# Rotary query columns of all heads projected ahead of the heads, plain query columns two heads at a time

## The chip, the cores and the metric

The kernel runs on one core of one Trainium2 chip. The metric is device microseconds for one execution, the lower the better. The core's engines are TensorE (PE, with PEld for its weight loads), VectorE (DVE), ScalarE (ACT), GpSimd (POOL) and SyncE (SP), which issues most DMAs. Each engine runs its own instructions in its own order, and they wait for one another by semaphores that count up.

## What is computed

The reference is one inference step of a two-layer decoder, for a prompt of 512 + 16 meta tokens and for 8 running samples of 4 new tokens each: 560 tokens in all. The first layer's mixer is multi-head latent attention with 16 heads, and only it is touched by the change:

```python
z = x @ w_in                                   # 1024 -> 384 + 256 + 32
cq = rms_norm(z[..., :384], q_norm)
ckv = rms_norm(z[..., 384:640], kv_norm)
kr = rope(z[..., 640:], pos)                   # one rotary key for all heads
q = (cq @ w_q_up).reshape(B, L, 16, 64 + 32)   # per head: 64 plain, 32 rotary columns
q_rope = rope(q[..., 64:], pos)
q_lat = einsum('blhn,chn->blhc', q[..., :64], w_uk)
s = (q_lat . c_kv + q_rope . k_rope) * 96 ** -0.5   # causal, then softmax, then times c_kv
```

`rope` takes the two halves x1, x2 of 32 columns to (x1 cos - x2 sin, x2 cos + x1 sin). The samples attend to 1024 cached positions, eight pages of 128 rows per sample, found through a page table. After the attention come its output projection, a SwiGLU channel mixer, an RG-LRU mixer and a second SwiGLU; they take the larger part of the time, and the change does not touch them.

## The kernel before

Activations are kept transposed, features on partitions and the 560 tokens along the row, in two halves of 280 (`toks`, `TH`). Products that need float32 precision are made as three fast products: operand and weight are each split into a rounded part and a remainder (`zqh`, `zql`; `wqh`, `wql`).

The attention of the prompt works by pairs of heads p = 0..7, each with a first head (u = 0) and a second head (u = 1). `pe ... head(p, u)` (L1155) is the order of TensorE's work, written out by hand: the scores of each block of 128 query rows (`scores`, L1071; block 4 is that of the 16 meta-end rows of both heads), transposes of earlier probabilities (`turn`, L1093), the products with the values of the head before (`outputs`, L1111), and, put in between, the projections for heads to come: `keys` (L1047), and `queries` (L1060), 18 matmuls of 280 columns per head: two token halves by three 128-row slices by three products. `queries` makes for one head a tile of 128 rows: 64 plain ones, the 32 rotary ones, and the same 32 once more with their halves swapped:

```python
# GpSimd, swap (L2725): the weights' halves swapped, then split
pool.tensor_copy(wq[u][:, :, 96:112], wq[u][:, :, 80:96]).then_inc(wq_sw, 1)
pool.tensor_copy(wq[u][:, :, 112:128], wq[u][:, :, 64:80]).then_inc(wq_sw, 1)
```

VectorE's `read_q` (L2194) multiplies the lower 64 rows by `trig` (cos and signed sin, scaled), ScalarE's `read_q` (L1668) copies the plain rows with the scale and, for the sample tokens, into `Qs`. `Q[u]` then holds 128 rows, and its product with `K[u]` (64 plain key rows, and the rotated rotary key `krs` twice) sums up the score in one matmul. The weights of a head's queries are loaded by SP into one of two tiles `wq[0]`, `wq[1]`, so that one can be loaded and split while the other is in use.

SP's program is one list. Around the attention it is: the loads of the front; the pages of samples 0 and 1 and the rotary pages of sample 0, as soon as VectorE's parameter steps are done (L574); after that the numbers of pages 2 and 3; the pages of sample 2; `pair_weights(0)` (L586), which waits for TensorE's transpose of `wuk` (`wt_sum`) and for each `queries` (`q_sum`) and loads the next pair's weights; the pages of sample 3; and then a loop with `pair_weights(i)` and the rotary pages of one sample (`sample_ropes`, L565) in each step. `numbers(b)` (L555) loads eight page numbers from SBUF into registers, once before each set of page loads. After the loop come the pages of samples 4 to 7.

GpSimd's list, in the heads: `values` (L2734) copies a head's values, `rotary` (L2738) gathers the sample columns of `Q`, `swap` prepares query weights, `key_weights` (L2744) key weights, `rows_out` (L2712) stores the latent rows, with four DMA issues for two tiles.

After the last head, TensorE needs the gathered sample queries (`qrot`) spread by a small matmul with `spread` (L1233), and it transposes the cached pages (`fill`, L1134). `fill(0, 4)` is the first to need rotary pages, and waits until those of all eight samples have come (`in_rp`).

Of the kernel before, what the change touches and what calls it, by code (L numbers as in the profile page):

```python
# [15 lines left out]
F32 = mybir.dt.float32  # L16
# [7 lines left out]
P = 128  # L24
# [107 lines left out]
def trunk(nc, x_prompt, x_sample, cache_latent, cache_krope, page_table, state_lru_h, state_conv, meta_tokens,  # L132
          mla_w_in, mla_q_norm, mla_w_q_up, mla_kv_norm, mla_w_uk, mla_w_uv, mla_w_o,
          lru_w_in, lru_conv_w, lru_conv_b, lru_w_a, lru_b_a, lru_w_i, lru_b_i, lru_lambda, lru_w_o,
          ffn_w_gu, ffn_w_down, ln_g, ln_b, c_ident, c_trig, c_mask, c_smask,
# [3 lines left out]
    with ExitStack() as ctx:  # L139
# [58 lines left out]
        wq = [put(f"wq{s}", [P, KQ, P]) for s in range(2)]  # L198
# [8 lines left out]
        rt = put("rt", [32, 2, T])  # L207
# [14 lines left out]
        wql = [place(f"wql{s}", [P, KQ, P], F32R, wq_at + 4 * KQ * P * s)[0] for s in range(2)]  # L222
        wqh = [place(f"wqh{s}", [P, KQ, P], F32R, raw_at + 4 * (PAGES * KV_R + KQ * P * s))[0] for s in range(2)]
# [6 lines left out]

        Ctok = [put(f"Ctok{s}", [P, PAGES, KV_R]) for s in range(2)]
        RP = put("RP", [P, B, PAGES, ROPE])
        Ctok += [raw[s][:, 0:PAGES * KV_R].rearrange("p (n c) -> p n c", n=PAGES) for s in range(2)]
# [9 lines left out]
        spt = put("spt", [P, 6, KD])  # L243
        zn = put("zn", [P, KC, NS])
# [246 lines left out]
        def _(sp):  # L491
# [41 lines left out]
            sp.dma_start(trig[:], c_trig).then_inc(in_att, 16)  # L533
# [13 lines left out]
            for u in range(2):  # L547
                sp.dma_start(wq[u][:, :, 0:hw], wqv[:, :, hw * u:hw * u + hw]).then_inc(wq_in[u], 16)
            for r in (64, 96):
                sp.dma_start(spread[r:r + 32, :].rearrange("p (a c) -> p a c", a=4),  # L550
                             c_ident[0:32, 0:32].rearrange("p (a c) -> p a c", a=1).broadcast_to([32, 4, 32])
                             ).then_inc(in_att, 16)
# [22 lines left out]
            sp.wait_ge(in_pg, 16)  # L575
            for b in range(2):
# [8 lines left out]

            def pair_weights(i):  # L586

                for u in range(2):
                    if u == 0:
                        sp.wait_ge(wt_sum, i + 1)  # L590
                        sp.dma_start(wuk[:], wukv[:, :, bass.ds(i * P + P, P)]).then_inc(wuk_in, 16)
                    sp.wait_ge(q_sum, i * 2 + (u + 1))
# [2388 lines left out]
```

## Time and profile before

| | |
|---|---|
| time, median of 3 runs | 1311.28 us (1310.70 to 1313.13) |
| the profiled execution's own time | 1310.86 us |
| its span, first to last instruction | 1309.0 us |
| TensorE busy | 1290.5 us, 99% of the span |
| VectorE busy | 883.3 us, 67% |
| ScalarE busy | 619.5 us, 47% |
| GpSimd busy | 279.5 us, 21% |
| granted TensorE clock, mean | 0.999 |

Busy times are for one execution. The heads lie between about 73 and 235 us; what follows the attention begins at about 300 us. In the profile's rows a line begins with its start and length in us, then engine, line of the kernel, operation, the tile written and those read, the shape and the number of instructions merged; in brackets stands the idle time of the engine before it and what ended it. "PE ps L1066" means TensorE writing to the accumulator memory for line 1066. A busy TensorE has overlapping matmuls, so a matmul's own length is more than the distance to the next.

### The profile page before, as it was taken

The page shows a single profiled execution, that of the slowest core. Times are in us where ns is not written, and L with a number is a line of the kernel's source. Part 1 is how long each engine was busy: PE and PEld are TensorE (multiplying, and loading weights), DVE is VectorE, ACT ScalarE, POOL GpSimd, SP SyncE. Part 2 cuts the span into 40 slices and gives each one's busy share as a digit, 9 for nine tenths or more (in the row PEclk, how much of TensorE's full clock was granted, in tenths as well). Part 3 has the DMA queues.
Part 4 walks back from the last instruction along what each step waited for, and adds up shares of the span by engine and source line. Part 5 has one row for each costly group of instructions (what it writes and reads, how often), then busy time and mean ns, then how long its engine had stood idle before and what let it go on. Part 6 is the DMA issues. An engine that isn't in the chain of part 4 may idle for free.

```text
span 1309.0 us, 26890 instructions
## 1 busy us (share of the span) xinstructions
PE 1290.5 (99%) x9985; PEld 1215.5 (93%) x9985; DVE 883.3 (67%) x1326; ACT 619.5 (47%) x1061; POOL 279.5 (21%) x391
## 2 busy tenths in 40 slices
PE   9999999999999999999999999999999999999997
PEld 9877777669999999999999899999999999999997
DVE  5766676433868478478864868888784784788646
ACT  4456666332555244144433488854552441444333
POOL 1243322001510000001104415645200000111034
PEclk9999999999999999999999999999999999999999
DMA  7231110342242655557752214222425655577501
GB/s 228 69 111 26 30 30 9 97 131 65 65 129 71 153 134 139 149 124 167 172 164 73 73 37 108 65 78 85 125 74 150 140 136 149 126 162 172 176 14 69
DMA packets 210088, 139.97 MB, mean 107 GB/s; under 512 B 27096, under 2 KB 198701, under 8 KB 210000
## 3 DMA queue, kind: packets, MB, share of 16 engines
q1 hardware_dynamic: 199616, 119.11, 31.9%
q0 software_dynamic: 10384, 19.67, 9.0%
q8 instruction: 58, 0.95, 0.3%
q14 instruction: 30, 0.25, 0.1%
HBM read 116.85 MB, written 3.02 MB: 92 GB/s over the span
## 4 chain that ended last, share of the span: by engine, by line
PE 78%; DVE 7%; ACT 5%; DMA 3%; issue 3%; POOL 2%; SPq 0%; DVEq 0%; POOLq 0%; ACTq 0%
PE ps L699 23%; PE ps L738 21%; PE ps L777 6%; PE ps L842 4%; PE ps L1079 3%; PE ps L1066 3%; DMA raw<-raw 2%; DVE wl L2044 2%; DMA raw<-in_ffn_w_gu 2%; PE ps L1102 1%; PE ps L1248 1%; PE ps L1290 1%; PE ps L914 1%; PE ps L1452 1%; PE ps L1312 1%
## 5 line engine op out<-in xcount | busy, mean ns | idle before, releaser
L738 PE MATMUL ps<-Th,wh 128*128 128x280 f32 x576 | 167.9, 292 | 0.0
L738 PE MATMUL ps<-Th,wl 128*128 128x280 f32 x576 | 167.5, 291 | 0.0
L738 PE MATMUL ps<-Tl,wh 128*128 128x280 f32 x576 | 167.2, 290 | 0.0
L2847 POOL DMA_DIRECT2D raw<-raw x36 | 42.9, 1192 | 531.3 <-DMA raw<-in_ffn_w_gu 531.3
L1540 ACT ACTIVATE wh<-raw 128x2048 fp32r<-128x2048 f32 (+4 forms) x50 | 92.3, 1846 | 122.2 <-PE ps L699 112.7
L2044 DVE TENSOR_TENSOR wl<-raw,wh 128x2048 fp32r<-128x2048 f32 (+4 forms) x50 | 113.2, 2264 | 31.9 <-ACT wh L1540 31.8
L738 PE MATMUL ps<-xl,wh 128*128 128x280 f32 x432 | 126.4, 293 | 0.0
L738 PE MATMUL ps<-xh,wh 128*128 128x280 f32 x432 | 125.9, 292 | 0.0
L738 PE MATMUL ps<-xh,wl 128*128 128x280 f32 x432 | 125.7, 291 | 0.0
L699 PE MATMUL ps<-hh,wh 128*128 128x280 f32 x512 | 107.9, 292 | 1.5 <-DVE wl L2044 1.5
L738 PEld LDWEIGHTS ps<-Th,wh 128*128 128x128 f32 x576 | 108.3, 188 | 0.0
L738 PEld LDWEIGHTS ps<-Th,wl 128*128 128x128 f32 x576 | 108.2, 188 | 0.0
L738 PEld LDWEIGHTS ps<-Tl,wh 128*128 128x128 f32 x576 | 108.2, 188 | 0.0
L699 PE MATMUL ps<-hl,wh 128*128 128x280 f32 x512 | 107.7, 292 | 0.0
L699 PE MATMUL ps<-hh,wl 128*128 128x280 f32 x512 | 107.5, 291 | 0.0
L1901 ACT ACTIVATE wh<-raw 128x512 fp32r<-128x512 f32 x36 | 22.8, 633 | 130.2 <-DVE w_s L2523 127.9
L699 PEld LDWEIGHTS ps<-hh,wh 128*128 128x128 f32 x512 | 81.1, 188 | 2.0 <-DVE wl L2044 2.0
L699 PEld LDWEIGHTS ps<-hh,wl 128*128 128x128 f32 x512 | 81.5, 189 | 0.0
L738 PEld LDWEIGHTS ps<-xh,wh 128*128 128x128 f32 x432 | 81.3, 188 | 0.2 <-DVE wl L2535 0.2
L738 PEld LDWEIGHTS ps<-xh,wl 128*128 128x128 f32 x432 | 81.4, 188 | 0.0
L699 PEld LDWEIGHTS ps<-hl,wh 128*128 128x128 f32 x512 | 81.1, 188 | 0.0
L738 PEld LDWEIGHTS ps<-xl,wh 128*128 128x128 f32 x432 | 81.1, 188 | 0.0
(442 smaller groups left out, 3649.0 us busy)
## 6 DMA issues: line engine op xcount, KB each, us to landing
raw<-in_ffn_w_gu SPq DMA_DIRECT2D x140, 256.0 KB, 4.7
raw<-in_ffn_w_gu SPq DMA_DIRECT2D x36, 512.0 KB, 4.1
raw<-raw POOLq DMA_DIRECT2D x36, 512.0 KB, 5.1
raw<-in_ffn_w_down SPq DMA_DIRECT2D x48, 256.0 KB, 3.1
raw<-in_lru_w_in SPq DMA_DIRECT2D x16, 512.0 KB, 4.9
Ctok<-in_cache_latent SPq DMA_DIRECT2D x48, 128.0 KB, 2.3
raw<-in_ffn_w_down SPq DMA_DIRECT2D x16, 384.0 KB, 3.7
raw<-in_mla_w_o SPq DMA_DIRECT2D x16, 256.0 KB, 3.6
```

Of the source, the lines that this page charges most:

```text
L699: mm = pe.matmul(ps[:, 1024 * jp + 512 * h:1024 * jp + 512 * h + TH], w[:, k, col:col + P], side(x, k, h), start=(k == 0 and n == 0), stop ...
L738: mm = pe.matmul(bank_of(bank), a, b, start=(k == 0 and m == 0), stop=(k == 3 and m == 2))
L777: mm = pe.matmul(bk(at), w[:, k, col:col + P], side(x, k, h), start=(k == 0 and n == 0), stop=(k == K_ - 1 and n == 2))
L842: return pe.matmul(bk(2 * (t + s) + h), w[:, k, P * s:P * s + P], x[:, k, toks(h)], start=(k == 0 and i == 0), stop=(k == KD - 1 and i == 2))
L914: return pe.matmul(ps[:, at:at + cols.stop - cols.start], w[:, k, jp * P:jp * P + P], x[:, k, cols], start=start, stop=stop)
L1066: mm = pe.matmul(ps[:, 512 * n:512 * n + TH], w[u][:, k, :], x[:, n * TH:(n + 1) * TH], start=(k == 0 and i == 0), stop=(k == KQ - 1 and i ...
L1079: pe.matmul(ps[:, bank:bank + w], Q[u][:, P * i:w], K[u][:, 0:w], start=True, stop=False)
L1102: mm = pe.transpose(ps[:, bank + j * P:bank + j * P + P], Pr[u][:, PR_AT[i] + j * P:PR_AT[i] + j * P + P], ident[:])
L1540: act.activation(wh[u][:, start:w], raw[u][:, start:w], ACT.Copy).then_inc(hi_ok, 1)
L1901: act.activation(quarters(wh[1], 0), quarters(raw[u], 0), ACT.Copy)
L2044: dve.tensor_tensor(wl[u][:, start:w], raw[u][:, start:w], wh[u][:, start:w].bitcast(F32), ALU.subtract).then_inc(lo_ok, 1)
L2847: pool.dma_start(quarters(raw[u], 3, 2), quarters(raw[u], 0, 3)[:, 0:3:2, :], accum_op=ALU.add).then_inc(r_out, 16)
```

## The change

The rotary columns of four heads at a time (32 each, 128 rows) are projected ahead of the first head, in four groups, and kept in four tiles `ropes`. From then on a projection makes the plain columns of two heads (2 x 64 rows), once per pair: half of its matmuls in the first head of the pair before, half in the second. The rotation's halves are no longer swapped in the queries: `Q[u]` gets rows 64 to 95 as `ropes` times cos, and rows 96 to 127 as `ropes` times sin, both made by GpSimd, and the lower rows of `K[u]` hold the rotated key and the key turned by a quarter. VectorE makes this second key with four more small products. Only one `wq` tile is left. SP loads the rotary columns in 12 small DMAs into space that pages use later, so the pages of samples 0 and 1 wait for their projection (`s_zms`), and the sines share space with the last rotary pages, so the rotary pages of samples 5 to 7 wait for the last rotary step (`q_rot`).

The core of the diff (tiles' places, constants, and the changes in semaphores' counts are cut):

```diff
             sp.wait_ge(s_xt, 10)
+            for g in range(4):
+                for k in range(KQ):
+                    sp.dma_start(wr[:, g, k, :].rearrange("p (h c) -> p h c", h=4),
+                                 wqv[:, k, 4 * hw * g:4 * hw * (g + 1)].rearrange("p (h c) -> p h c", h=4)[:, :, NOPE:hw]
+                                 ).then_inc(pg_in[4], 16)
...
+            sp.dma_start(sines[:], c_trig[2 * P:3 * P, :]).then_inc(pg_in[4], 16)
             sp.wait_ge(in_pg, 16)
+            def pair_weights(i):
+
+                sp.wait_ge(q_sum, i + 1)
+                for s in range(2):
+                    sp.dma_start(wq[:, :, NOPE * s:NOPE * s + NOPE],
+                                 wqv[:, :, bass.ds(i * (2 * hw) + (2 + s) * hw, NOPE)]).then_inc(wq_in[0], 16)
+                sp.wait_ge(wt_sum, i + 1)
+                sp.dma_start(wuk[:], wukv[:, :, bass.ds(i * P + P, P)]).then_inc(wuk_in, 16)
+
+            pair_weights(0)
+            sp.wait_ge(s_zms, 6)
             for b in range(2):
                 pages_b = numbers(b)
                 sample_pages(b, pages_b)
...
             pages_23 = [numbers(b) for b in (2, 3)]
             sp.wait_ge(s_v, 8)
             sample_pages(2, pages_23[0])
...
-            pair_weights(0)
+            pair_weights(1)
             sample_pages(3, pages_23[1])
             sample_ropes(1, numbers(1))
-            with sp.Fori(1, HEADS // 2 - 1) as i:
+            sample_ropes(2, numbers(2))
+            for i in range(2, HEADS // 2 - 1):
                 pair_weights(i)
-                sample_ropes(i + 1, numbers(i + 1))
+                if i < 4:
+                    sample_ropes(i + 1, numbers(i + 1))
+            sp.wait_ge(q_rot, 3 * HEADS)
+            for b in range(5, B):
+                sample_ropes(b, numbers(b))
             pages_45 = [numbers(b) for b in (4, 5)]
...
+            def rope_queries(g, at):
+
+                for n in range(2):
+                    for k in range(KQ):
+                        for i, (w, x) in enumerate(((wrh, zqh[k][:]), (wrh, zql[:, k, :]), (wrl, zqh[k][:]))):
+                            mm = pe.matmul(ps[:, 512 * (at + n):512 * (at + n) + TH], w[:, g, k, :], x[:, toks(n)],
+                                           start=(k == 0 and i == 0), stop=(k == KQ - 1 and i == 2))
+                mm.then_inc(s_zms, 1)
...
-                    if i == 4:
-                        if last:
-                            fill(0, 0)
-                            fill(0, 1)
-                        else:
-                            queries(h + 1, v, 0)
+                    if i == 4 and last:
+                        fill(0, 0)
+                        fill(0, 1)
...
-                    if i == 3 and u == 0:
-                        queries(h + 1, v, 0)
-                if not last:
-                    if u == 1:
-                        pe.wait_ge(ql_rd, p + 1)
-                    queries(h + 1, v, 1)
-                else:
+                if u == 0 and more:
+                    queries(p + 1, 0)
+                elif u == 1 and not last:
+                    pe.wait_ge(ql_rd, p + 1)
+                    queries(p + 1, 1)
+                elif last:
                     fill(0, 2)
                     fill(0, 3)
...
+            rope_queries(0, 4)
+            pe.wait_ge(s_ve, 5)
+            pe.wait_ge(s_vd, 5)
+            rope_queries(1, 2)
+            rope_queries(2, 0)
+            pe.wait_ge(s_zroot, 8)
+            rope_queries(3, 4)
...
             def read_q(p):
+                dve.wait_ge(q_sum, p + 1)
+                dve.tensor_scalar(halves(Q[1][0:NOPE, :]), pair(0, 64, P), SCALE, None, ALU.mult)
...
+                dve.tensor_scalar(Qs[64:P, NS:2 * NS], ps[64:P, 512 + TH - NS:512 + TH], SCALE, None, ALU.mult).then_inc(q_dve, 1)
...
+            def split_queries(p):
+
+                pool.wait_ge(wq_in[0], 32 * p + 32)
+                pool.tensor_copy(wqh[:], wq[:]).then_inc(wq_sw, 1)
+                pool.wait_ge(wq_sw, 2 * p + 3)
+                pool.tensor_tensor(wql[:], wq[:], wqh[:].bitcast(F32), ALU.subtract).then_inc(wq_sw, 1)
...
+            def rotary(h):
+
+                p, u, g, rows = h // 2, h % 2, h // 4, slice(32 * (h % 4), 32 * (h % 4) + 32)
+                pool.wait_ge(s_zinv if g % 2 else s_zroot, 3 + g // 2 if g % 2 else 8 + g // 2)
+                if p > 0:
+                    pool.wait_ge(sc_sum, scored(p - 1, 1, 3 if u else 4))
...
+                pool.tensor_tensor(Q[u][64:96, :], ropes[g][rows, :], trig[rows, :], ALU.mult).then_inc(q_rot, 1)
+                pool.wait_ge(q_rot, 3 * h + 1)
+                pool.tensor_tensor(Q[u][96:P, :], ropes[g][rows, :], sines[rows, :], ALU.mult).then_inc(q_rot, 1)
+                pool.wait_ge(q_rot, 3 * h + 2)
+                pool.tensor_copy(qrot[64:P, :, h:h + 1, :].rearrange("p b a t -> p b (a t)"),
+                                 Q[u][64:P, NP:T].rearrange("p (b t) -> p b t", t=TS)).then_inc(q_rot, 1)
...
+            rotary(0)
             for t in range(2, 4):
                 rows_out(t)
+            rotary(1)
+            split_queries(1)
             key_weights(1)
             for h in range(1, HEADS):
+                if h < HEADS - 1:
+                    rotary(h + 1)
                 if h == 1:
                     for t in range(4, 6):
                         rows_out(t)
                 elif h % 2 == 0 and h < HEADS - 2:
+                    split_queries(h // 2 + 1)
                     key_weights(h // 2 + 1)
                 if h < HEADS - 1:
                     pool.wait_ge(o_sum, h * 2)
                     values(h + 1, 1 - h % 2)
```

## Rows read from the trace of the kernel before

**Rows 1.** Stretches: busy us of PE, PEld, DVE, ACT, POOL; PEclk; DMA share; GB/s.

```profile
3.00:4.00 1.00, 1.00 (x7) 1.00 (x7) 0.00 (x0) 0.00 (x0) 0.00 (x0) 1.00 0.61 168
...
8.00:9.00 1.00, 1.00 (x12) 1.00 (x11) 0.66 (x3) 0.42 (x2) 0.00 (x0) 1.00 0.99 400
...
92.00:112.00 20.00, 20.00 (x158) 15.75 (x159) 13.55 (x36) 12.78 (x39) 6.84 (x18) 1.00 0.14 31
```

**Rows 2.** The chain of waits, end of a first head and start of a second.

```profile
96.04 2.31 PE ps L1066 x18
...
99.96 0.97 PE ps L1083 x4
...
101.56 1.15 PE ps L1066 x9
```

**Rows 3.** Timeline of PE: pair 0, and the first head of pair 1.

```profile
73.32 0.46 PE L1079 MATMUL ps<-K,Q 128*128 128x128 f32 x2
...
76.66 0.38 PE L1066 MATMUL ps<-zqh,wqh 128*128 128x280 f32 x1
...
80.24 1.04 PE L1083 MATMUL ps<-K,Q 128*16 128x512 f32 x4 [0.23 <-ACT Qs L1676]
...
91.84 0.49 PE L1079 MATMUL ps<-K,Q 128*128 128x128 f32 x2
...
98.28 0.44 PE L1122 MATMUL ps<-PT,Vs 128*64 128x264 f32 x1
```

**Rows 4.** Timelines of DVE (the first row) and ACT (the other two).

```profile
49.04 1.82 DVE L2147 TENSOR_TENSOR rt<-ps,trig 32x280 f32<-32x280 f32 x4
...
97.43 0.59 ACT L1655 ACTIVATE PT<-ps 128x512 f32<-128x512 f32 x1
...
101.86 0.70 ACT L1647 ACTIVATE Pr<-ps,mx 80x528 f32<-80x528 f32 x1 [0.97 <-DVE mx L2179]
```

**Rows 5.** Timeline of POOL.

```profile
28.69 1.40 POOL L2704 TENSOR_TENSOR zsq<-zsq 128x560 f32<-128x560 f32 x1 [1.04 <-ACT zsq L1597]
...
73.67 0.54 POOL L2722 DMA_DIRECT2D out<-lat  x1 [3.36 <-ACT lat L1619]
...
91.98 0.40 POOL L2735 COPY Vs<-V 128x256 f32<-128x256 f32 x1 [6.15 <-PE ps L1131]
...
96.66 0.51 POOL L2730 CAST wqh<-wq 128x384 fp32r<-128x384 f32 x1
97.26 1.01 POOL L2732 TENSOR_TENSOR wql<-wq,wqh 128x384 fp32r<-128x384 f32 x1
```

**Rows 6.** Timeline of SP's queue: DMA issues.

```profile
41.39 4.03 SPq L562 DMA_DIRECT2D Ctok<-in_cache_latent  x8
45.61 4.40 SPq L567 DMA_DIRECT2D RP<-in_cache_krope  x8
54.62 3.95 SPq L562 DMA_DIRECT2D Ctok<-in_cache_latent  x8
67.95 4.75 SPq L562 DMA_DIRECT2D raw<-in_cache_latent  x8
74.09 0.39 SPq L591 DMA_DIRECT2D wuk<-in_mla_w_uk  x1
...
88.38 4.05 SPq L567 DMA_DIRECT2D RP<-in_cache_krope  x8
...
235.10 9.20 SPq L562 DMA_DIRECT2D Ctok<-in_cache_latent  x16
```

**Rows 7.** DMA issues from 20 to 200 us: size and median us to landing.

```profile
wq<-in_mla_w_q_up SPq DMA_DIRECT2D x16, 144.0 KB, 2.4
```

**Rows 8.** Timeline of PE: pair 7 begins; transposes of rotary pages and of pages 4.

```profile
209.85 0.49 PE L1079 MATMUL ps<-K,Q 128*128 128x128 f32 x2
...
229.63 0.60 PE L1152 MATMUL ps<-ident,RP 128*128 128x128 f32 x4
...
249.31 1.09 PE L1152 MATMUL ps<-ident,Ctok 128*128 128x128 f32 x8
```

More of the change, by code:

```diff
@@ L197, in trunk @@
         wq_at = put.at()
-        wq = [put(f"wq{s}", [P, KQ, P]) for s in range(2)]
+        wq = put("wq", [P, KQ, P])
+        put("wq_pad", [P, KQ, P])
         wuk = put("wuk", [P, KC, P])
@@ L221, in trunk @@
         zqh = [place(f"zqh{k}", [P, T], F32R, at)[0] for k, at in enumerate((stat_at, ring_end - 3072, rt_at))]
-        wql = [place(f"wql{s}", [P, KQ, P], F32R, wq_at + 4 * KQ * P * s)[0] for s in range(2)]
-        wqh = [place(f"wqh{s}", [P, KQ, P], F32R, raw_at + 4 * (PAGES * KV_R + KQ * P * s))[0] for s in range(2)]
+        wql = place("wql", [P, KQ, P], F32R, wq_at)[0]
+        wqh = place("wqh", [P, KQ, P], F32R, raw_at + 4 * PAGES * KV_R)[0]
+        ktrig = place("ktrig", [P, T], F32, qlat_at + 4 * 2 * (KV_R + ROPE))[0]
+        sines = place("sines", [P, T], F32, LIMIT - 4 * T)[0]
+        ropes = [place(f"ropes{g}", [P, T], F32, at)[0] for g, at in enumerate((
+            xh_at + 16 * T, xh_at + 4 * KD * T + 16 * T, xh_at + 20 * T, stat_at + 4 * T))]
         wuvh = place("wuvh", [P, KC, HEADS * VH], F32R, raw_at + 4 * W_MAX)[0]
@@ L229, in trunk @@
         kvh, kvl = (t[:, KD - KC:KD, :] for t in (xh, xl))
+        ctok_at = put.at()
         Ctok = [put(f"Ctok{s}", [P, PAGES, KV_R]) for s in range(2)]
+        rp_at = put.at()
         RP = put("RP", [P, B, PAGES, ROPE])
+        wr, wrh, wrl = (place(n, [P, 4, KQ, P], dt, at)[0] for n, dt, at in (
+            ("wr", F32, ctok_at), ("wrh", F32R, ctok_at + 4 * PAGES * KV_R), ("wrl", F32R, rp_at)))
         Ctok += [raw[s][:, 0:PAGES * KV_R].rearrange("p (n c) -> p n c", n=PAGES) for s in range(2)]
@@ L574, in _ @@
             sp.wait_ge(s_par, 26)
+            sp.dma_start(sines[:], c_trig[2 * P:3 * P, :]).then_inc(pg_in[4], 16)
             sp.wait_ge(in_pg, 16)
+            def pair_weights(i):
+                sp.wait_ge(q_sum, i + 1)
+                for s in range(2):
+                    sp.dma_start(wq[:, :, NOPE * s:NOPE * s + NOPE],
[4 more added lines that the diff above has]
+            sp.wait_ge(s_zms, 6)
             for b in range(2):
@@ L1158, in head @@
                 last = isinstance(h, int) and h == HEADS - 1
+                more = not isinstance(p, int) or p < HEADS // 2 - 1
                 if u == 0:
@@ L1222, in _ @@
                 row_tile(t)
-            with pe.Fori(0, HEADS // 2 - 1) as i:
+            with pe.Fori(0, HEADS // 2 - 2) as i:
                 head(i, 1)
                 head(i + 1, 0)
+            head(HEADS // 2 - 2, 1)
+            head(HEADS // 2 - 1, 0)
             head(HEADS // 2 - 1, 1)
@@ L1717, in head @@
                         act.activation(wukT[:], ps[:, 0:KV_R], ACT.Copy).then_inc(wt_rd, 1)
-                if not last:
-                    read_q(p + u, v)
+                if u == 1 and not last:
+                    read_q(p + 1)
                 if not first:
@@ L2256, in head @@
                     fills(0, (1,))
-                elif not (isinstance(h, int) and h == 0):
-                    read_q(h + 1, v)
+                elif u == 1:
+                    read_q(p + 1)
             read_k(0)
-            read_q(0, 0)
+            read_ropes(1, 1)
+            read_ropes(3, 2)
+            read_q(0)
             for u in range(2):
@@ L2751, in key_weights @@
                 pool.tensor_tensor(wukl[:], wuk[:], wukh[:].bitcast(F32), ALU.subtract).then_inc(s_kp2, 1)
-            for u in range(2):
-                pool.wait_ge(wq_in[u], 16)
-                swap(u, u)
+            split_queries(0)
             key_weights(0)
@@ L2944, in constants @@
     rot = np.concatenate([cos, cos, -sin, sin], axis=0)
-    trig = np.concatenate([rot, rot * np.float32(SCALE)], axis=0).astype(np.float32)
+    keys = np.concatenate([rot, cos, -cos, sin, sin], axis=0)
+    queries = np.concatenate([np.tile(t, (8, 1)) * np.float32(SCALE) for t in (cos, sin)], axis=0)
+    trig = np.concatenate([keys, queries], axis=0).astype(np.float32)
+    turn = np.zeros((ROPE, ROPE), np.float32)
+    turn[np.arange(half), np.arange(half) + half] = 1
+    turn[np.arange(half) + half, np.arange(half)] = -1
     q, k = np.arange(P)[:, None], np.arange(P)[None, :]
```

138 lines of the change are left out of this document (61 added, 77 removed).

## The prediction

> **What bounds the kernel now.** I read by stage, since shares over 1309 us say nothing of one. The table of stretches [rows 1] shows TensorE busy for all of 92 to 112 us, a stretch of the heads, with 13.55 us of VectorE, 12.78 of ScalarE and 6.84 of GpSimd beside it. That looks like a pure TensorE limit, and each of the 16 heads spends 18 matmuls on its queries, 0.128 us apart (18 in 2.31 [rows 2]). The chain of waits, read with what ScalarE does at the same moments, corrects this. In a second head of a pair, the nine query matmuls at 101.56 end at 102.71 [rows 2]; the scores behind them need the exponential of the meta rows, which runs 101.86 to 102.56 [rows 4]. In a first head the values' product ("outputs") starts at 98.28 [rows 3], and what it reads, the turned probabilities, is copied out by ScalarE from 97.43 to 98.02 [rows 4]. So in both places the query matmuls fill a gap that would be there without them. Last I read SP, which issues the loads in its own order: eight page numbers cost 4.61 us (50.01 to 54.62), eight page loads 3.95 to 4.75, eight small rotary-page loads 4.05 to 4.40, none of it waiting [rows 6].
>
> Below, E(p) is the time at which pair p begins (its first head's scores). E(1) = 91.84 and E(7) = 209.85 [rows 3, 8], so a period is 19.67, of which the first head takes 8.12 (to 99.96 [rows 2]) and the second 11.55.
>
> **The change, in order of time.**
>
> (a) Ahead of the heads. 72 matmuls for four groups of rotary columns are added: 72 x 0.128 = 9.2. VectorE turns the keys with eight products where four took 1.82 [rows 4]; up to 1.8 more, 0 if its idle time takes it up; I take 0.3, as what waits for it comes many operations later. A second small query copy must end before the first scores: 0.2. First scores: 73.32 [rows 3] becomes 83.0. The 12 new weight loads and the split of these weights lie in 27 to 50 us, where SP and GpSimd stand idle and TensorE only needs them at 70: nothing, and up to 1 if they are late.
>
> (b) Pair 1's plain queries in the first head. TensorE reaches them 3.34 after the scores begin [rows 3], at 86.4. GpSimd, though, now does in this order: rows out of tiles 2 and 3 (four issues of 0.54, starting 0.35 after the first scores [rows 3, 5]), so to 85.5; then the rotary rows of head 1; then the split. The rotary step is new: two products of 32 partitions by 560 and one small copy. The trace has 128 x 560 at 1.40 [rows 5]; with 32 partitions it costs between a quarter of that and 1.40. I take 1.40, as a quarter of the lanes idle needs no less time for the same 560 elements; 2 x 1.40 + 0.21 and three waits of 0.08 make 3.25. The split is 0.51 + 0.09 + 1.01 = 1.61 [rows 5]. So 90.4: a stall of 4.0. Behind it nine matmuls stand, where 18 stood. The second head begins at 92.8 against 80.24 [rows 3]: **+12.5**. (The Trainium skill, GPSIMD Engine Reference, section 2, gives every core 16 fixed partitions, by which 32 partitions save nothing; the trace has no case of it.)
>
> (c) The second head of pair 0 keeps its length: nine matmuls go, but the scores behind them wait for the same exponential. E(1) becomes 104.3.
>
> (d) SP's order. This is the largest term. The next pair's query weights used to be loaded between the pages; now SP waits for the queries of pair 0, loads pair 1's weights, waits for the transpose of wuk (it issued that load 0.77 after the first scores, and took 0.39 [rows 3, 6]), so is free at 84.2, and only then starts on the pages that before were done from 36 us on: numbers 4.61, then 17.18 (41.39 to 58.57: pages 0, rotary pages 0, numbers, pages 1), two sets of numbers and a wait that took 9.38 (58.57 to 67.95), pages 2 4.75: 35.9. At 120.1 comes the load of pair 2's weights, in two parts: 0.45 later the second, 2.4 to land [rows 7], split 1.61: 124.6. TensorE wants them at E(1) + 3.95, 108.3. **A stall of 16.3.** Queries 1.15, a gap 0.1, outputs 1.68 (98.28 to 99.96): the second head begins at 127.5 against 99.96, so +27.5, 15 more than in (b). ScalarE, VectorE and GpSimd all wait behind it.
>
> (e) Pair 3. E(2) = 127.5 + 11.55 = 139.0. SP from 121.0: wuk 0.39, pages 3 4.0, then twice numbers and rotary pages (2 x 8.66) end at 142.7, weights and split 145.5 and 147.1. GpSimd alone would be ready at E(2) + 5.6 = 144.7 (see f). The second head starts at 150.1 against 119.63: +30.5, another 3.0.
>
> (f) Pairs 3 to 6, first head. Loads are in time. GpSimd copies the values from 0.14 after E (0.40 [rows 5], and an estimated 0.17 more for the second, smaller copy), does a rotary step (3.25), and then the split (1.61): E + 5.6, where TensorE wants it at 3.95. Its nine matmuls end at 6.8, and outputs start at 6.9 instead of 6.44: +0.45 four times, 1.8. The removed half of the matmuls buys nothing. Pair 7 has no queries to make: outputs wait for the copy, E + 6.2: -0.25. E(7) = 209.85 + 32.0.
>
> (g) The last rotary pages, 5 to 7, wait until GpSimd's last rotary step, E(7) + 4.0. Three times 8.66 = 26.0; with landing (2.4 at most [rows 7]; I take 1.7 after the last issue starts) E(7) + 31.5. TensorE's first transposes of the rotary pages, which need all of them, came at 229.63 [rows 8], E(7) + 19.8, now 19.5: **a stall of 12.0**. Pages 4 and 5 come 2.5 later against TensorE than before; their loads ran 235.10 to 244.30, landed by 246.7 and were needed at 249.31 [rows 6, 8]: nothing, at most 1.
>
> (h) Restart. At the start of the kernel, after standing idle, TensorE did 7 matmuls in the fourth microsecond, and 12 in the ninth [rows 1], both at a granted clock of 1.00, its upper level. Some 3.5 us at 7 in place of 12 lose 1.5. I charge it at the two long stalls, 3.0; nothing at least, and 2.9 at each of four stalls at most (queries, outputs at half the pace). The Trainium skill (TensorE: Matmul & The Clock Gate, "HAM oscillation") says that idle gaps drop the engine to its lower clock, and that the next work starts cold. By it the term is real, though none of this trace's rows inside the heads has such a gap.
>
> **Sum.** 12.5 + 15.0 + 3.0 + 1.8 - 0.25 + 12.0 = 44.0, with (h) 47. The profiled execution took 1310.86, the median is 1311.28, so it stands for the runs. Forecast 1358.
>
> **Rivals.**
> - *Restart dear.* Every one of the four stalls costs 2.9: 44 + 11.6, 1367. Chance 0.10.
> - *TensorE bound after all.* Seven second heads each gain their nine matmuls, 1.15, as the exponential of the meta rows comes earlier when VectorE has less to do: 1350. Against it: its end, 102.56, hangs on the scores' own end. 0.08.
> - *Tail hidden.* (g) isn't on the path, the rotary pages overlapping with something I missed: 1346. 0.06.
> - *Faster: the work counts, the loads come in time.* TensorE makes 72 matmuls fewer (288 to 216): -9.2, 1302. It needs SP to reach pair 2's weights before 106 and not 120, so its run of 35.9 to be under 22, and the stalls of (b) to be covered too. The rows of SP leave no idle time in that run to take out. 0.03.
> - *The change doesn't do what it says*: the matmuls are issued all the same, or the steps overlap so that nothing shows: 1311. 0.01.
>
> **Numbers.** The forecast has 0.72. Its range: half the price of a rotary product takes 1.4 from (b), 1.8 from (f) and 1.4 from (g)'s start, no restart takes 3, small loads 1, so about 1349; up, dear restarts and late pages reach 1368. This leaves out the tail case and the two small ones, 0.10. Faster and slower mean by over 0.2%, about what a measurement tells: 0.03 and 0.96, between 0.01.
>
> **What would show it.** Right: the query weights of pair 2 issued at about 120 us, TensorE idle for some 16 us before a projection, a second gap of 12 before the transposes of the rotary pages, and each first head's split landing after TensorE asks for it. GpSimd's 32 x 560 products at 1.4. Wrong: page numbers that take much less than 4.6 a set, or query weights loaded before the pages.

## The result and the profile after

| | before | after |
|---|---|---|
| time, median | 1311.06 us (1310.62 to 1313.13, 6 runs) | 1360.40 us (1359.32 to 1361.52, 6 runs) |
| ratio | | 1.0374 [1.0364, 1.0384] |
| profiled execution, its span | 1310.86, 1309.0 us | 1359.32, 1357.5 us |
| TensorE busy | 1290.5 us, 99% | 1291.6 us, 95% |
| GpSimd busy | 279.5 us, 21% | 312.0 us, 23% |
| mean granted clock | 0.999 | 0.984 |

TensorE issues 72 matmuls fewer (9913 for 9985) and is yet busy 1.1 us longer than before, partly because some of its work ran at the lower clock (below); the other 47.4 of the 48.5 us between the spans are idle time. All readings of the kernel after are of one profiled execution, the fastest of the six (1359.32). Where the idle time lies, the waits of TensorE in the stretch of the heads and the tail show (60 to 290 us; in a row the waiting line, its releaser, then us in total, times, longest):

```profile
PE ps L1096 <- POOL wql L2782: 27.8, 7, 16.2
PE ps L1182 <- DMA RP<-in_cache_krope: 10.1, 1, 10.1
PE ps L1109 <- ACT Pr L1687: 8.4, 9, 1.1
PE ps L1152 <- ACT PT L1695: 2.3, 1, 2.3
```

The first line is the query projection that waits for the split weights (steps b, d, e, f), the second the transposes of the rotary pages (g). The third is the gap that the nine removed query matmuls filled in a second head: they took 1.15 us [rows 2], and 1.1 us of idle stands there instead.

TensorE's timeline after, with the rows that answer to [rows 3, 8] (start, length, and in brackets the idle before):

```profile
82.44 0.46 PE L1109 MATMUL ps<-K,Q 128*128 128x128 f32 x2 [0.30 <-DVE Qs L2241]
89.87 0.60 PE L1096 MATMUL ps<-zqh,wqh 128*128 128x280 f32 x1 [3.91 <-POOL wql L2782]
93.40 1.04 PE L1113 MATMUL ps<-K,Q 128*16 128x512 f32 x4
...
125.42 0.60 PE L1096 MATMUL ps<-zqh,wqh 128*128 128x280 f32 x1 [16.22 <-POOL wql L2782]
130.73 1.04 PE L1113 MATMUL ps<-K,Q 128*16 128x512 f32 x4
...
148.04 0.40 PE L1096 MATMUL ps<-zqh,wqh 128*128 128x280 f32 x1 [1.52 <-POOL wql L2782]
151.01 1.04 PE L1113 MATMUL ps<-K,Q 128*16 128x512 f32 x4
...
188.63 0.40 PE L1096 MATMUL ps<-zqh,wqh 128*128 128x280 f32 x1 [1.52 <-POOL wql L2782]
189.98 0.44 PE L1152 MATMUL ps<-PT,Vs 128*64 128x264 f32 x1
...
243.78 0.49 PE L1109 MATMUL ps<-K,Q 128*128 128x128 f32 x2
250.23 0.70 PE L1152 MATMUL ps<-PT,Vs 128*64 128x264 f32 x1 [2.26 <-ACT PT L1695]
...
275.34 1.09 PE L1182 MATMUL ps<-ident,RP 128*128 128x128 f32 x4 [10.13 <-DMA RP<-in_cache_krope]
...
297.00 1.09 PE L1182 MATMUL ps<-ident,Ctok 128*128 128x128 f32 x8
```

SP's queue after, against [rows 6]:

```profile
81.28 0.90 SPq L597 DMA_DIRECT2D wq<-in_mla_w_q_up  x2
83.21 0.37 SPq L600 DMA_DIRECT2D wuk<-in_mla_w_uk  x1
89.07 4.01 SPq L572 DMA_DIRECT2D Ctok<-in_cache_latent  x8
93.26 4.64 SPq L577 DMA_DIRECT2D RP<-in_cache_krope  x8
102.59 3.94 SPq L572 DMA_DIRECT2D Ctok<-in_cache_latent  x8
115.89 3.95 SPq L572 DMA_DIRECT2D raw<-in_cache_latent  x8
119.89 0.97 SPq L597 DMA_DIRECT2D wq<-in_mla_w_q_up  x2
...
143.04 0.96 SPq L597 DMA_DIRECT2D wq<-in_mla_w_q_up  x2
...
252.37 21.44 SPq L577 DMA_DIRECT2D RP<-in_cache_krope  x24
```

The weights of pair 2 go out at 119.89, after every page from sample 0 to 2. The spaces between the issues are page numbers: 102.59 less 97.90 is 4.69 us for eight. Against time of before, the marks that the two traces share stand so:

| mark | before | after | later by | forecast |
|---|---|---|---|---|
| first scores | 73.32 | 82.44 | 9.1 | 9.7 |
| second head of pair 0 | 80.24 | 93.40 | 13.2 | 12.5 |
| second head of pair 1 | 99.89 | 130.73 | 30.8 | 27.5 |
| second head of pair 2 | 119.56 | 151.01 | 31.4 | 30.5 |
| first scores of pair 7 | 209.85 | 243.78 | 33.9 | 32.0 |
| first rotary page transposes | 229.63 | 275.34 | 45.7 | 44 |
| last transposes of that part | 249.31 | 297.00 | 47.7 | 44 + restart |
| end of the span | 1309.0 | 1357.5 | 48.5 | 47 |

The marks are rows of the timelines; the prediction took 99.96 and 119.63 for two of them from the chain of waits, 0.07 later than the timeline, which changes no step.

The granted clock in four stretches after (from and to, length, PE busy with its matmuls, granted clock, DMA share, GB/s):

```profile
116.00:124.00 8.00, 0.00 (x0) 0.50 0.72 201
126.00:130.00 4.00, 4.00 (x24) 0.50 0.27 87
130.00:132.00 2.00, 2.00 (x20) 0.84 0.10 16
276.00:280.00 4.00, 4.00 (x19) 0.50 0.02 4
```

0.50 is the lower of the two levels, 1.2 GHz. TensorE had stood idle from 109.2 to 125.4 and did more than its first four microseconds of work at that level. The chain of waits prices it, with the same nine matmuls at either level behind the DMA that ended the stall:

```profile
120.36 3.30 DMA wq<-in_mla_w_q_up
...
125.42 2.47 PE ps L1096 x9
...
159.91 1.16 PE ps L1096 x9
```

### The profile page after: what moved, and what is told of

Read it like the earlier page. It is cut to its first block, busy times and chain, and to the rows that moved or that the text cites. A ratio compares the mean times of both kernels' runs of the same rounds, so it can differ in the third digit from the quotient of the medians.

```text
span 1357.5 us, 26559 instructions
## 1 busy us (share of the span) xinstructions
PE 1291.6 (95%) x9913; PEld 1213.2 (89%) x9913; DVE 883.2 (65%) x1332; ACT 614.2 (45%) x1047; POOL 312.0 (23%) x377
## 3 DMA queue, kind: packets, MB, share of 16 engines
HBM read 117.42 MB, written 3.02 MB: 89 GB/s over the span
## 4 chain that ended last, share of the span: by engine, by line
PE 74%; DVE 7%; issue 4%; SPq 4%; ACT 4%; DMA 4%; POOL 4%; POOLq 0%; DVEq 0%; ACTq 0%
PE ps L720 22%; PE ps L759 21%; PE ps L798 7%; PE ps L863 4%; SPq L566 2%; DVE wl L2086 2%; DMA raw<-raw 2%; DMA raw<-in_ffn_w_gu 2%; PE ps L1096 1%; PE ps L1109 1%; PE ps L1182 1%; PE ps L1288 1%; PE ps L1330 1%; SPq L577 1%; PE ps L935 1%
```

## The experiments

The theory: the time is lost to the order of two hand-written lists (SP's and GpSimd's) and to the projections ahead of the heads, and the matmuls removed inside the heads stood in gaps and were worth nothing. The rival: TensorE's own work is the bound, so that with the lists mended the change wins its 9 us.

**sp_order**, one part alone: SP's weight loads ahead of the pages of their step. (Not shown: the loop behind, in which the weights of pair 4 now come after two sets of rotary pages.)

```diff
             for b in range(2):
                 pages_b = numbers(b)
+                if b == 1:
+                    pair_weights(1)
                 sample_pages(b, pages_b)
...
             sample_pages(2, pages_23[0])
-            pair_weights(1)
+            pair_weights(2)
             sample_pages(3, pages_23[1])
```

> The changed kernel with SP's list reordered alone: pair 2's weights are loaded before the pages of sample 1, pair 3's before the pages of sample 3. My theory (the idle stretch of 16.2 us before pair 1's first head ends is SP's queue, and it drags the TensorE clock down): the stretch shrinks to about 2 us, what GpSimd's own order leaves, and the 2.9 us of half-speed matmuls behind it mostly go: 1360.4 - 14.5 - 2.5 = about 1343, with no new long gap at the next pair. Rival 1 (the loads only change places, the pages or the next weights are late instead): a gap of 10 us or more reappears later, 1355 to 1360. Rival 2 (the clock is a reading of the profile and costs nothing): 1346.

Measured: 1345.48 (1343.44 to 1348.33), ratio 1.0267 [1.0250, 1.0284]. TensorE's waits, 60 to 290 us:

```profile
PE ps L1100 <- POOL wql L2786: 14.5, 7, 3.9
PE ps L1186 <- DMA RP<-in_cache_krope: 11.6, 1, 11.6
```

and the query projections of pair 1's and pair 3's first heads:

```profile
110.62 0.40 PE L1100 MATMUL ps<-zqh,wqh 128*128 128x280 f32 x1 [1.46 <-POOL wql L2786]
...
152.69 0.40 PE L1100 MATMUL ps<-zqh,wqh 128*128 128x280 f32 x1 [3.02 <-POOL wql L2786]
```

The stall of 16.2 has become one of 1.46, and the queries and outputs behind it take 2.97 us (110.62 to 113.59) for 5.31: at the second head of pair 1 the trace stands 17.1 earlier than the changed kernel's, as the theory said. 14.9 of time was won, 2.5 less than expected. Two losses in the trace come behind: pair 4's weights are late, a wait of 3.02 where 1.52 is usual, and the tail's stall grew by 1.5, as the rotary pages 5 to 7 keep their own chain from the last rotary step on. The median lies at Rival 2's number (1346, a clock that costs nothing), but the 2.97 for 5.31 speak against it: the clock costs, and two other losses took as much.

**tail_numbers**: the page numbers of the last rotary pages are read ahead of the wait for GpSimd's last rotary step.

```diff
+            pages_57 = [numbers(b) for b in range(5, B)]
             sp.wait_ge(q_rot, 3 * HEADS)
             for b in range(5, B):
-                sample_ropes(b, numbers(b))
+                sample_ropes(b, pages_57[b - 5])
```

> The changed kernel, with the numbers of the pages of samples 5 to 7 read ahead of the wait for the last rotary step, in SP's idle time; the loads stay where they are. My theory (the 10.1 us before the transposes of the rotary pages are three sets of page numbers, 13.8 us, in a row with the loads): the gap closes entirely, and the half-speed stretch behind it goes: 1360.4 - 10.1 - 2 to 3 = 1347 to 1348. Rival (the loads themselves are late, their 24 issues after the last rotary step): the gap shrinks by less than 5, 1355 or more.

Measured: 1347.40, ratio 1.0277 [1.0260, 1.0295]. The wait for the rotary pages has left the list of waits, and their 24 loads now follow one another:

```profile
247.85 12.58 SPq L577 DMA_DIRECT2D RP<-in_cache_krope  x24
```

12.58 us where the changed kernel's took 21.44: the rest was page numbers, which wait for nothing. Here 13.0 us were won, more than the stall of 10.1, as the half-speed stretch behind it is gone too.

**numbers_early**: the numbers of pages 0 and 1 are read before `pair_weights(0)`, while SP stands waiting.

```diff
+            pages_01 = [numbers(b) for b in range(2)]
             pair_weights(0)
             sp.wait_ge(s_zms, 6)
             for b in range(2):
-                pages_b = numbers(b)
+                pages_b = pages_01[b]
```

> The changed kernel, with the page numbers of samples 0 and 1 read into registers before SP waits for the first queries, in idle time. My theory (SP's list is the path from 84 to 120 us, and a set of numbers takes 4.6 us of it): 2 x 4.6 = 9.2 us off the 16.2 us stall, and the half-speed stretch behind it stays as some 7 us of idleness are left: 1351. Rival (the numbers overlap with the DMA issues, or the weights wait for something else): less than 3 us won.

Measured: 1351.50, ratio 1.0297 [1.0281, 1.0313], as expected. The longest wait for the split fell from 16.2 to 5.2 us. So it is the length of SP's list, not the transfers, that sets the stall.

**gps_order**: GpSimd splits the query weights ahead of the rotary rows, and does the rotary step of head 1 ahead of the row stores.

```diff
             for h in range(1, HEADS):
+                if h % 2 == 0 and h < HEADS - 2:
+                    split_queries(h // 2 + 1)
+                    pool.wait_ge(wq_sw, h + 6)
                 if h < HEADS - 1:
                     rotary(h + 1)
```

> The changed kernel, with GpSimd's list reordered alone: in each pair the query weights are split before the next head's rotary step, and head 1's rotary step goes ahead of the row stores. My theory: the waits of TensorE for the split, 3.9 us at pair 1 and 1.6 us at each of five pairs after the long stall, go to below 1 and to 0; but behind the 1.6 us only about 0.6 is won per pair, as the values' product then waits for the turned probabilities. 3.2 + 1 of clock + 5 x 0.6 = 7: 1353, while SP's stall stays. Rival (all of the waits is won): 3.9 + 5 x 1.6 + clock = 13: 1347. Rival (nothing, since rotary steps become late instead): 1360.

Measured: 1360.91 (1360.57 to 1362.48), ratio 1.0376 [1.0359, 1.0394]: a miss of 8, no gain at all. TensorE's waits:

```profile
PE ps L1096 <- POOL wql L2782: 21.6, 3, 19.2
...
PE ps L1152 <- ACT PT L1695: 9.3, 5, 2.3
```

Three things took the gain in this trace. What pair 1 won went into the next stall, 19.2 for 16.2, because SP's list sets its end. That the theory should have said. And in the steady pairs the wait for the split is gone, but another of 1.7 to 1.8 us stands in its place: the values' product waits for ScalarE's copy of the turned probabilities. 1.1 of that stands wherever nine query matmuls are missing from a first head (no_gap_first, below); the other 0.6 to 0.7 is new. And in pair 5 the granted clock fell to 0.50 (214 to 218 us) behind such a wait of 1.79, which made that pair's second head 2.1 longer; behind the equal waits of pairs 3, 4 and 6 it did not. Two rows, GpSimd's and VectorE's, say what makes the copy late:

```profile
185.21 1.00 POOL L2782 TENSOR_TENSOR wql<-wq,wqh 128x384 fp32r<-128x384 f32 x1
...
185.43 0.86 DVE L2229 TENSOR_SCALAR Pr<-Pr,rsum 128x128 f32<-128x128 f32 x1
```

VectorE's normalising of one block takes 0.29 in the kernel before. Here it takes 0.86 and ends at 186.29, 0.08 after GpSimd's instruction. The column maximum of the last block then starts 0.64 later in the head than before (4.82 us after its first scores for 4.18), and ScalarE's last copy with it (6.22 for 5.59).

**port_products** puts that to the test in the kernel before: two products of 32 x 560 more on GpSimd, in seven first heads, into a tensor that nobody reads any more. Nothing waits for them. They took 1.11 us each.

```diff
+                if h % 2 == 1 and h < HEADS - 1:
+                    pool.wait_ge(v_cp, 2 * h + 4)
+                    for n in range(2):
+                        done[0] += 1
+                        pool.tensor_tensor(krs[0:32, :], stat[64:96, 1, :], stat[64:96, 1, :],
+                                           ALU.mult).then_inc(s_zinv, 1)
+                        pool.wait_ge(s_zinv, 2 + done[0])
```

> The kernel before with two more GpSimd products of 32 x 560 in each of seven first heads, on tensors that nobody waits for, so that GpSimd only runs beside VectorE's normalising of the probabilities. Theory (the products stretch VectorE's work from SBUF to SBUF, and the values' transposes wait for it, 0.5 to 0.6 a pair): 1315 (1314 to 1316). Rival, the stretch is hidden: 1311.4.

Measured: 1316.97 (1316.33 to 1317.31), ratio 1.0039 [1.0024, 1.0053], against 1312.01 on the same chip: 5.0 us, 0.7 a pair. That is a little above the theory's 1314 to 1316 and far from the rival's 1311.4. The timelines of GpSimd, VectorE and TensorE in one first head, merged by time:

```profile
195.32 2.30 POOL L2793 TENSOR_TENSOR krs<-stat 32x560 f32<-32x560 f32 x2
...
196.60 1.11 DVE L2187 TENSOR_SCALAR Pr<-Pr,rsum 128x128 f32<-128x128 f32 x1
...
201.71 0.41 PE L1122 MATMUL ps<-PT,Vs 128*64 128x264 f32 x1 [0.67 <-ACT PT L1655]
```

Again the VectorE instruction ends 0.09 after GpSimd's (197.71 and 197.62), and the wait of 0.67 stands in each of the seven pairs (the list of waits has 4.7 us, 7 times). It is what gps_order had beyond its 1.1. The same group by form, 91.77 to 230 us, in the kernel before and then in this one (busy us, mean ns of one, idle before):

```profile
L2187 DVE TENSOR_SCALAR Pr<-Pr,rsum 128x128 f32<-128x128 f32 x14 | 4.0, 286 | 0.5
```

```profile
L2187 DVE TENSOR_SCALAR Pr<-Pr,rsum 128x128 f32<-128x128 f32 x14 | 9.8, 698 | 0.5
```

So an engine that is busy a fifth of the time costs 5 us through an instruction on another engine that never reads its results. The Trainium skill (SBUF — State Buffer, "Who interferes with whom") describes it as a lock on a port pair that VectorE and GpSimd share, held for a whole instruction: the loser "**fully blocks**". The ends 0.08 and 0.09 behind GpSimd's agree with that.

**no_gap_second** leaves out of the kernel before nine of the 18 query matmuls in seven heads, those that run in the second head of a pair; those query tiles are not computed.

```diff
                 if n == 0:
                     pe.wait_ge(wq_sw, h * 4 + 4)
+                    if u == 0 and (not isinstance(h, int) or h > 0):
+                        return
```

> The kernel before, without the first nine query matmuls for each next pair, those in the middle of seven second heads; their result is left out, so the scores of half of the tokens are computed from what stands in the accumulator. All else stays. My theory (they fill a gap, the scores behind them wait for the exponential of the meta rows): 7 x 0.05 = 0.3 us faster, 1310.7 to 1311. Rival (TensorE bounds the heads): 7 x 1.15 = 8 us faster, 1303.

Measured: 1313.05 (11 runs), ratio 1.0012 [1.0003, 1.0022]: no gain, if anything 1.7 us slower, where 0.3 faster was expected. In the trace every pair begins within 0.04 us of before, so the difference lies behind the heads; its cause is open. **no_gap_first** leaves out the nine of each first head in the same way (`if u == 1`).

> The kernel before, without the first nine of the 18 query matmuls in each of the eight first heads (their result is left out). My theory (the values' product waits for ScalarE's copy of the turned probabilities, 0.25 us before the matmuls end): 7 x 0.25, and up to 1.1 in the first pair that has no such product, 2 to 3 us faster, about 1308.5. Rival (TensorE bounds the heads): 8 x 1.15 = 9.2 us faster, 1302.

Measured: 1310.65 (11 runs), ratio 0.9995 [0.9986, 1.0004]: 0.7 us faster than before on the same chip, not clear of nothing, and a miss, as 2 to 3 were expected. In the trace the first head of pair 0 is 1.0 shorter (5.92 for 6.92), as expected; the 0.25 in each of the seven others did not come. The waits of TensorE in the two, second first:

```profile
PE ps L1081 <- ACT Pr L1649: 8.4, 9, 1.1
```

```profile
PE ps L1124 <- ACT PT L1657: 7.5, 7, 1.1
```

Nine matmuls are 1.15 us of work; without them 1.1 us of idle appears, on ScalarE both times. TensorE looked 100% busy there [rows 1], and 7 x 1.15 = 8.1 us of its work could be removed for nothing, in the second heads or in the first. Each was removed alone; both waits stand side by side in all_three, where both sets are gone. So the change has no gain inside the heads to set against its costs.

**all_three**: the edits of sp_order, tail_numbers and gps_order together.

> The three reorderings together, nothing left out. My theory: what stays is the price of the four groups ahead of the heads, 9.2 us of TensorE, and the halved query matmuls win next to nothing, since they lay in gaps that ScalarE's and VectorE's chain leaves open: 1311 + 9.2 + 0.7 for the first pair - 1 = about 1320 (1317 to 1324). Rival (TensorE bounds the heads, so 144 matmuls fewer there count, 18 us): 1302 to 1306. So the sign against the kernel before is what decides.

Measured: 1328.69 (1327.61 to 1331.82), ratio 1.0136 [1.0119, 1.0153]. The rival's 1302 to 1306 is out, and the theory's number is 8.7 too low. 3.6 us are a wait of pair 4, whose weights stood in SP's list behind two sets of rotary pages, and 1.5 more went to the lower clock behind it (4.49 us of queries and outputs for 2.96); the others are five waits for ScalarE's copy (9.0 us), as in gps_order. Not all of that is lost time: 1.1 us of each stand where the removed matmuls were, and a steady pair is 0.6 longer than before.

**best_order** mends the first (weights of pairs 3 and 4 ahead of the rotary pages) and moves both rotary steps of a pair into the second head before it, so that the split alone stands in the first head.

```diff
             for h in range(1, HEADS):
-                if h < HEADS - 1:
+                if h % 2 == 1 and h < HEADS - 1:
                     rotary(h + 1)
+                    rotary(h + 2)
...
                     split_queries(h // 2 + 1)
+                    pool.wait_ge(wq_sw, h + 6)
                     key_weights(h // 2 + 1)
```

> The changed kernel with SyncE's weight loads ahead of the pages of their head for pairs 1 to 4, the tail's page numbers ahead of the last rotary pages, and GpSimd's list turned over: both rotary steps of the next pair stand in the second head before the values, and the split stands first and alone in the first head. Theory (the lists cost the time, and GpSimd's products beside VectorE's normalising cost some 0.6 a pair): from the 1328.7 of all_three take the 3.6 that pair 4 still waited for its weights, about 1 of restarts, and 0.6 for each of five or six pairs, which gives about 1320 (1317 to 1324). Rival, the rotary products stretch VectorE's work wherever they stand: 1325 to 1328. Rival, TensorE's own work is the bound, so that the nine matmuls taken from each second head are won: 1302 to 1306. By the theory it stays slower than the kernel before, since the matmuls ahead of the heads cost 9 and those taken away gave nothing.

Measured: 1325.99 (1325.11 to 1329.44), ratio 1.0111 [1.0093, 1.0130]: within the first rival's range, outside the theory's. Its waits:

```profile
PE ps L1160 <- ACT PT L1703: 9.7, 5, 2.0
...
PE ps L1104 <- POOL wql L2790: 3.6, 3, 1.4
```

and two of its rows, in a first head that has no rotary product:

```profile
183.61 1.00 POOL L2790 TENSOR_TENSOR wql<-wq,wqh 128x384 fp32r<-128x384 f32 x1
...
183.83 0.86 DVE L2237 TENSOR_SCALAR Pr<-Pr,rsum 128x128 f32<-128x128 f32 x1
```

As in gps_order, it is the split that meets the normalising, for the same 0.86, and here the split of the key weights meets the next one too. The rotary products now run in the second heads, which last as long as before (11.60 to 11.62 for 11.6), so the first rival's number came out but not its reason: there the stretch is hidden. In the kernel before, the query split comes at 96.66 to 98.27 [rows 5], after the maxima that matter. It is the fastest variant of the change, and 14.0 us slower than the kernel before on the same chip. In its trace the pairs begin 9.2 later at pair 0 and 13.0 later at pair 7 (pairs 1 and 2 cost 0.5 each, pairs 3 to 6 0.8 each, and pair 0 gives 0.5 back); 2.6 us more lie behind the heads, and I did not trace them.

**front_more**: the fourth group of rotary columns (number 3, counted from 0) is projected twice, 18 matmuls of 280 columns more (the expectation says the third group and 128 columns).

```diff
             pe.wait_ge(s_zroot, 8)
+            rope_queries(3, 4, False)
             rope_queries(3, 4)
```

> The changed kernel with the third group of rotary columns projected twice ahead of the heads, 18 more matmuls of 128 columns. Theory (work ahead of the heads is on the path at its full length, and SyncE's list moves with it): 18 x 0.128 = 2.3 more, 1362.7. Rival, it is hidden beside the loads of the first pages: 1360.4.

Measured: 1362.00 (1360.91 to 1362.79), ratio 1.0378 [1.0361, 1.0395], where the changed kernel has 1.0374 [1.0364, 1.0384]. The intervals overlap, so the time does not tell the theory from the rival. The traces say more. tail_numbers has the same lists up to the tail, and against it the first scores come 1.58 later (85.22 for 83.64), SP's weights of pair 2 1.56 later (121.85 for 120.29), and the stall before them is the same (14.57 for 14.58): what is added ahead of the heads passes in full through SP's list. How much was added the traces can't give: with the same work ahead of them, the first scores lie between 82.34 and 83.95 in the executions of the changed kernel and its variants.

**warm_stall** and **warm_55** fill the stall of pair 2 with warming matmuls, 120 and 55 calls, to price the restart.

```diff
+                if warm_it:
+                    warm(120)
                 if u == 0 and more:
                     queries(p + 1, 0)
```

> The changed kernel, with 120 matmuls of 128 columns on constants put in front of the queries in pair 1's first head, where TensorE stands idle for 16.2 us; 120 need some 13 us at full clock, so they end before the weights are there. My theory (the clock, 0.50 in that stretch and until 131 us, costs what the 5.3 us of matmuls behind the stall last more than 2.8 at full clock): about 2.5 us faster although 120 matmuls are added, 1358, and a granted clock of 1.00 behind the stall. Rival (the half clock is hidden behind other engines): same time, 1360.4. Rival (they delay the queries): slower.

Measured: 1368.53, ratio 1.0435 [1.0419, 1.0451]. The calls:

```profile
110.29 26.96 PE L952 MATMUL ps<-ones 128*128 128x128 f32 x240
```

They ran to 137.0, past the arrival of the split weights (126.2), and delayed the queries: a call is two matmuls and takes 0.22 us, and I had sized it at half. The granted clock was 1.00 from 108 to 142, and the queries and outputs behind the calls took 2.94 us (137.01 to 139.95) for 5.31. So the restart's price is shown, 2.4, but the time is no test of what taking it away would win.

> The changed kernel with 55 warming calls (two matmuls each, about 13 to 15 us by the earlier run's 0.25 a call) in the stall of pair 2 before its query matmuls. Theory (the restart at half clock behind that stall costs 2.5 to 3): the clock stays at 1.00 and the time is 1357.5 (1357 to 1358.5). Rival, the restart is hidden or only moved: 1360.4. If the calls run past the arrival of the weights, later than 1360.4 by what they run over.

Measured: 1361.83 (1361.51 to 1362.08), ratio 1.0380 [1.0363, 1.0397], no gain, at the rival's number. The stretches (columns as above):

```profile
110.00:122.00 12.00, 12.00 (x110) 1.00 0.30 88
126.00:128.00 2.00, 2.00 (x10) 0.52 0.71 234
...
150.00:152.00 2.00, 2.00 (x16) 0.50 0.10 15
```

The calls ended at 122.6, 3.0 us before the split weights, and the clock fell to 0.52 all the same, later: queries and outputs took 4.52 us (125.55 to 130.07) for 5.31. TensorE so reached pair 2 0.65 us earlier, and there it waited longer for pair 3's weights, 2.57 for 1.52, as SP sent them at 143.90. Behind that wait the clock fell again, at 150, where the changed kernel had 1.00. So what the calls won was lost again, and more, at the next stall. A kernel that keeps the clock up through the whole stall was not tried.

## Why the prediction was right, and where its steps were off

The forecast was 1358; the median is 1360.4. The mechanism held at each large step, and the rivals fell: the two no_gap runs and all_three exclude that TensorE's work is the bound, tail_numbers' 13 us exclude a hidden tail, the second scheme in which the loads come in time gave 1326 at best, and the restarts cost less than 11.6.

- **(a)** 9.7 forecast, 9.1 measured in this execution; in the variants with the same work there the first scores come 9.0 to 10.6 later than in the kernel before, so the tenths mean little. VectorE's eight products took 3.63 where four took 1.82 [rows 4], all of it hidden; I had charged 0.3. front_more's traces agree that work there is on the path, and in best_order, where nearly all stalls are gone, the 9.2 at the first scores are not won back.
- **(b)** GpSimd's order was right to the tenth: stall 3.91 for 4.0, products 1.36 each for 1.40. The queries started at 89.87 for 90.4, because of (a). What is too little in "+12.5" is restart, which (h) charged at the long stalls only: the granted clock was 0.50 here too, from 90 to 93 us, and the nine query matmuls took 2.27 (89.87 to 92.14) for 1.16. The prediction's "a quarter of the lanes idle" should read three quarters; the time it took from that, the full one, was right.
- **(c)** Right: the second head of pair 0 lasted 11.61 (93.40 to 105.01) for 11.60.
- **(d)** Right: the weights of pair 2 at 119.89 for 120.1, stall 16.22 for 16.3. The landing was mis-sized, 3.3 for 2.4 (the DMA row of the chain above), while the DMA engines' share was 0.72; that the pages before it are the reason is not shown.
- **(e)** This step failed: "another 3.0" was 0.6, what any steady pair costs by (f). SP did reach pair 3's weights at 143.04, as forecast at 142.7. But the long stall and its restart had delayed TensorE's pair 2 to 142.3 for the 139.0 of the forecast, and what is late already does not wait. Behind them GpSimd needed to 148.0 in any case. The 2.4 too much here and the 2.6 too little in (d) (17.6 measured for 15.0, restart included) nearly cancel: one delay, counted in two places. Where the first stall is shorter, the wait for SP does appear: in numbers_early the first head of pair 2 lasts 10.84 for 8.05, partly from its wait of 2.40 and partly from the lower clock behind it.
- **(f)** +0.45 forecast, 0.62 a pair measured. Queries start E + 5.71 for 5.6 and the outputs E + 7.06 for 6.9 (188.63 and 189.98, E = 182.92). GpSimd's list, as forecast, but its rows lie a little wider. VectorE's lateness is there too (the 128 x 128 normalising at 0.37 us mean for 0.29), only hidden: TensorE waits for the split longer. gps_order and port_products uncover it. Pair 7's gain of 0.25 did not come: outputs at E + 6.45.
- **(g)** Stall 10.1 for 12.0. The loads started and ran as forecast. The first transposes came at E(7) + 31.56 for 31.5, but TensorE reached them at E(7) + 21.4 for 19.5: pair 7's outputs (250.23 to 253.16) took 2.9 for 1.6 at the lower clock, and its 0.25 had not come. That lower clock does not come each time: in tail_numbers, behind the same wait of 2.26, the clock stayed at 1.00 and the outputs took 1.6. From pair 7's first scores to the transposes it is 11.8 more than before, with 12 forecast.
- **(h)** The term was under-sized: 3.0 for 5.4. At the long stall queries and outputs took 5.31 (125.42 to 130.73) where pair 5's took 2.96 (188.63 to 191.59), 2.3 more (warm_stall and sp_order, with 2.94 and 2.97, say the same); at pair 1's queries (b) it was 1.1; after the tail's stall 21.66 us passed for 19.68, 2.0. The Trainium skill's section named in (h) gives the direction, and the rows agree; the price comes from the rows alone. The one at pair 7 cost nothing, as the rotary pages were late.

The sum of the measured marks, 13.2 + 17.6 + 0.6 + 2.5 + 11.8 + 2.0, is 47.7, plus 0.8 behind. That the forecast is 2.4 off the median is the sum of errors of both signs, up to 3 us each: the mechanism was right, but that it came so close is in part luck.

Left open: where the last 0.8 us lie, what drops the clock behind a wait of about 2 us in one execution and not in another, and whether the idle of 1.1 us that the removed matmuls left could be filled with the rotary columns' projections. That was not tried. By the no_gap runs I estimate that it could at most take back the 9.1 ahead of the heads, which ends at the time of before.

## What to carry to other kernels

Before a change that removes work from a busy engine, remove that work alone and time it: here 8 us of matmuls were worth nothing, since another engine's chain set the end of each stretch. Write out every issue list that the change touches, each instruction that it moves past included (eight page numbers were 4.6 us), and put what the next stage waits for first. When several stalls follow one another, carry the delay of the first into the second before charging it again.

## What was not expected of the hardware

- A GpSimd instruction from SBUF holds up a VectorE `TENSOR_SCALAR` from SBUF to SBUF until it ends: 286 ns became 698 on the mean in port_products, its end 0.09 us behind GpSimd's in the row shown. `TENSOR_REDUCE` from the accumulator memory stayed at 0.29 and 0.42 us in the same heads.
- The clock falls and rises with a lag. In warm_55 it was still 1.00 up to 126 us, when TensorE had been idle for 3.0 us and was already working again, and 0.52 from 126 to 128. Idle stretches of 1.5 us, one a pair, left it at 1.00.
- Between 1.7 and 3.1 us of idle, the same wait does not always have the same effect. Behind the 2.26 us before pair 7's outputs the clock fell to 0.5 or 0.6 in the traces of the changed kernel, numbers_early, gps_order and warm_55, and stayed at 1.00 in those of sp_order, tail_numbers, all_three, front_more and warm_stall. A wait of 1.79 brought it down once in gps_order, and one of 3.02 in sp_order did not. These falls cost 0.9 to 2.1 us each in the length of their head, so readings of single traces differ by that.
